# Scale after the product: RMSNorm's token factor moved behind the matmuls of a two-layer trunk

## The reference

```
def _rmsnorm(x, g):
    y = xf * lax.rsqrt(jnp.mean(xf * xf, axis=-1, keepdims=True) + RMS_EPS)
    return y * g
for layer in range(2):
    h = _rmsnorm(x, norm_mix[layer])
    if layer == 0:
        q, k, v, g, alr, u, sv = split(h @ even_w_in)        # 1024 -> 2576
        m = concat(_gla(q, k, v, g, alr, ...), _sgu(u, sv, ...))
    else:
        p = h @ odd_w_in                                      # 1024 -> 2720
        m = concat(_rwkv7(p[..., :1696], ...), _conformer_conv(p[..., 1696:], ...))
    x = x + m @ w_out
    f = square(relu(_rmsnorm(x, norm_ffn[layer]) @ w_up[layer]))   # 1024 -> 4096
    x = x + f @ w_down[layer]
return _rmsnorm(x, norm_final)
```

## Time and profile before

| | us |
|---|---|
| three runs | 1438.53, 1440.8, 1441.72 (median 1440.8) |
| the profiled execution: its own time | 1437.61 |
| the profiled execution: span of its trace | 1435.8 |
| PE busy | 1307.3 (91%) |
| DVE busy | 688.4 (48%) |
| ACT busy | 420.4 (29%) |
| POOL busy | 449.4 (31%) |

### The profile page before, as it was taken

One profiled execution on the slowest core, in us unless ns is written; L12 is line 12 of the kernel. 1 busy time (PEld: TensorE's weight loads), 2 busy tenths in 40 slices (PEclk: granted clock), 3 DMA queues, 4 the chain that ended last, 5 costly groups with the idle time before them and its releaser, 6 DMA issues. The chain is left out here.

```text
span 1435.8 us, 20378 instructions
## 1 busy us (share of the span) xinstructions
PE 1307.3 (91%) x8452; PEld 1046.4 (73%) x8452; DVE 688.4 (48%) x972; ACT 420.4 (29%) x535; POOL 449.4 (31%) x101
## 2 busy tenths in 40 slices
PE   4998998999999999898798898777889999999997
PEld 3897976888888888675666556564668888888885
DVE  6226256541014421386868878686655410144213
ACT  4537222231113211262435223232322311132110
POOL 3332232444434544321121110110224444345441
PEclk9999998999999999899999987898989999999998
DMA  5331212222232223201001000000022222322221
GB/s 191 121 108 34 86 59 88 75 100 89 90 106 97 88 91 110 93 30 60 31 31 59 30 31 2 30 31 1 30 88 78 98 88 91 108 93 88 92 85 58
DMA packets 16802, 106.17 MB, mean 74 GB/s; under 512 B 1872, under 2 KB 2144, under 8 KB 4704
## 3 DMA queue, kind: packets, MB, share of 16 engines
q1 hardware_dynamic: 15872, 103.83, 21.1%
q10 hardware_dynamic: 864, 1.36, 0.3%
HBM read 103.09 MB, written 2.10 MB: 73 GB/s over the span
## 5 line engine op out<-in xcount | busy, mean ns | idle before, releaser
L410 POOL TENSOR_TENSOR w_lo<-w_raw,w_hi 128x2048 fp32r<-128x2048 f32 x94 | 444.7, 4731 | 949.9 <-ACT w_hi L476 362.0
L748 PE MATMUL ps<-h_hi,w_hi 128*128 128x512 f32 x792 | 324.7, 410 | 8.5 <-DVE h_lo L1199 4.1
L748 PE MATMUL ps<-h_lo,w_hi 128*128 128x512 f32 x792 | 313.2, 395 | 0.0
L748 PE MATMUL ps<-h_hi,w_lo 128*128 128x512 f32 x792 | 312.8, 395 | 0.0
L748 PEld LDWEIGHTS ps<-h_hi,w_hi 128*128 128x128 f32 x792 | 151.2, 191 | 59.1 <-issue 19.9
L476 ACT ACTIVATE w_hi<-w_raw 128x2048 fp32r<-128x2048 f32 x58 | 111.1, 1915 | 276.5 <-PE ps L748 204.2
L748 PEld LDWEIGHTS ps<-h_hi,w_lo 128*128 128x128 f32 x792 | 151.4, 191 | 32.8
L748 PEld LDWEIGHTS ps<-h_lo,w_hi 128*128 128x128 f32 x792 | 151.7, 192 | 31.4 <-issue 2.7
L1253 DVE TENSOR_TENSOR x<-x,ps 128x512 f32 (+1 forms) x32 | 22.0, 687 | 305.2 <-PE ps L748 233.7
L1236 DVE TENSOR_TENSOR f_hi<-relu 128x512 f32 x64 | 71.6, 1119 | 172.2 <-ACT relu L462 160.3
L748 PE MATMUL ps<-f_hi,w_lo 128*128 128x512 f32 x384 | 151.9, 396 | 0.0
(11 more groups left out here) (279 smaller groups left out, 1769.3 us busy)
## 6 DMA issues: line engine op xcount, KB each, us to landing
w_raw<-in_weights SPq DMA_DIRECT2D x94, 1024.0 KB, 4.9
outT<-x SPq DMA_DIRECT2D x8, 256.0 KB, 2.2
x<-in_xT ACTq DMA_DIRECT2D x4, 256.0 KB, 5.5
x<-in_xT SPq DMA_DIRECT2D x4, 256.0 KB, 5.3
masks_f<-in_masks SPq DMA_DIRECT2D x1, 768.0 KB, 12.9
low_w<-in_low_w SPq DMA_DIRECT2D x1, 512.0 KB, 13.7
sgu_ln<-in_sgu_ln SPq DMA_DIRECT2D x1, 512.0 KB, 3.4
sgu_w<-in_sgu_w SPq DMA_DIRECT2D x1, 256.0 KB, 3.9
```

Source lines behind the costliest of these rows:

```text
L410: pool.tensor_tensor(w_lo[:, j, :], w_raw[:, j, :], w_hi[:, j, :].bitcast(f32), SUB)\
L748: mm = pe.matmul(bank(gb(g) if isinstance(i, int) else g % 2), w, r, start=(k == 0 and m == 0), stop=(k == K - 1 and m == 2))
```

## The change

The token factor is one number per token, so a product of (x times weight) differs from the product of the normed input by that factor alone. The changed kernel cuts x times weight: ACT makes `h_hi` straight from `x` with the weight as scale (`h_cut`), DVE `h_lo` in one instruction (`h_rest`), tile by tile as `x` becomes final. The factor is applied to the results: in the MLP as its square, since relu(c u) squared is c\*c relu(u) squared (`rn` then holds 1 / mean square, and DVE multiplies each down tile by it before adding it to `x`); in layer 0 as ACT's scale for the token-major tiles, and for k and q on the decay factors; in layer 1 at each tile's way out of PSUM, where the mix with `mu` is written anew (DVE `psh`, ACT `dsh` = psh times (1 - mu), DVE the sum). `stat` and `spread` become steps of the order, behind the first products. `m_hi0` to `m_lo1` give the mixers' outputs memory of their own, since `h_hi` is now written while an output product still reads its operands; other tensors move, and many counters are merged. In the first 13 tiles of layer 0 the PSUM banks come from a list (`FIRST_BANKS`). The first loads come in another order, and chunk 0 is loaded and cut only in its first half, which is all that its one product reads.

```
-        ORDER1 = [("slice", t, q) for q in range(4) for t in (0, 2)] + quarters([4])[:2] + [("zw", 0)] \
+        ORDER1 = [("slice", t, q) for q in range(4) for t in (0, 2)] + [("stat",)] + quarters([4]) + [("spread",)] \
...
-            if step[0] == "slice" and step[2] == 3 and (step[1] < 14 or step[1] % 2):
-                held += [("evac_v", step[1])]
-            if held and "dx" not in [other[0] for other in ORDER1[at + 1:at + 4]]:
-                order += held
-                held = []
+            if step[0] == "slice" and step[2] == 3:
+                held += [step[1]]
+            scaled_yet = scaled_yet or step[0] == "spread"
+            coming = [other[0] for other in ORDER1[at + 1:at + 4]]
+            if not scaled_yet or "dx" in coming:
+                continue
+            for t in begun:
+                order += [("evac_b", t), ("low", t)]
+            begun = []
+            for t in held:
+                order += [("evac_a", t), ("evac_q", t)]
+                if t == held[-1] and t < 14 and coming[:1] in (["slice"], ["taps"]):
+                    begun += [t]
+                else:
+                    order += [("evac_b", t), ("low", t)]
+            held = []
...
+            for k in (0, 2):
                 sp.dma_start(x[:, k, :], xT_in[:, k, :]).then_inc(s(f"x_loaded{k}"), 16)
-            for n in range(2):
-                sp.dma_start(w_raw[:, n, :], weights[n, :, :]).then_inc(s(f"raw_loaded{n}"), 16)
+            sp.dma_start(w_raw[:, 0, 0:1024], weights[0, :, 0:1024]).then_inc(s("raw_loaded0"), 16)
+            for k in range(4, KD):
+                sp.dma_start(x[:, k, :], xT_in[:, k, :]).then_inc(s(f"x_loaded{k}"), 16)
+            sp.dma_start(w_raw[:, 1, :], weights[1, :, :]).then_inc(s("raw_loaded1"), 16)
+            sp.dma_start(mats[:, :, :], mats_in).then_inc(s("mats_loaded"), 16)
             sp.dma_start(masks_f[:, :], masks_in).then_inc(s("masks_loaded"), 16)
             sp.dma_start(low_w[:, :, :], low_w_in).then_inc(s("low_w_loaded"), 16)
             sp.wait_ge(s("lo_done"), 1)
             sp.dma_start(w_raw[:, 0, :], weights[2, :, :]).then_inc(s("raw_loaded0"), 16)
-            sp.wait_ge(s("h_ready"), KD)
+            sp.wait_ge(s("stat_done"), 1)
...
+            pool.tensor_tensor(w_lo[:, 0, 0:1024], w_raw[:, 0, 0:1024], w_hi[:, 0, 0:1024].bitcast(f32), SUB)\
+                .then_inc(s("lo_done"), 1)
+            pool.wait_ge(s("hi_done"), 2)
...
+            def spread(m):
+                act.wait_ge(s("spread_done"), m + 1)
+                act.activation(rn[:, :], bank(6), ACT.Copy).then_inc(s("rn_done"), 1)
+            def h_cut(m, k):
+                if m:
+                    act.wait_ge(*x_final(m, k))
+                else:
+                    act.wait_ge(s(f"x_loaded{k}"), 16)
+                act.activation(h_hi[:, k, :], x[:, k, :], ACT.Copy, scale=col(NORMS[m], k)).then_inc(s("h_hi_done"), 1)
...
+                    elif layer == 0:
+                        for d in range(KD):
+                            if d < KD - 1:
+                                cut_hi(nd + 2 + d)
+                            h_cut(2, d)
+                        cut_hi(nd + 2 + KD - 1)
...
+            act.dma_start(cols[:, :], cols_in).then_inc(s("cols_loaded"), 16)
+            for k in (1, 3):
                 act.dma_start(x[:, k, :], xT_in[:, k, :]).then_inc(s(f"x_loaded{k}"), 16)
...
+            h_cut(0, 0)
+            h_cut(0, 1)
+            act.wait_ge(s("raw_loaded0"), 16)
+            act.activation(w_hi[:, 0, 0:1024], w_raw[:, 0, 0:1024], ACT.Copy).then_inc(s("hi_done"), 1)
+            for k in range(2, KD):
+                h_cut(0, k)
+            cut_hi(1)
...
+                act.wait_ge(s("gemm_done"), g + 1 + (g % 2 if kind == "v" else 0))
+                if kind == "v":
+                    act.wait_ge(s("rrms_done"), 1)
...
                 fn = {"v": ACT.Copy, "sv": ACT.Gelu_apprx_tanh, "u": ACT.Gelu_apprx_tanh, "g": ACT.Silu}[kind]
-                act.activation(dst[:, t, 256 * half:256 * half + 256], bank(g % 2, 0, 256), fn)\
-                   .then_inc(s(f"gemm_evac{g % 2}"), 1)
+                act.activation(dst[:, t, 256 * half:256 * half + 256], tok_bank(g), fn, scale=rrms[:, t:t + 1])\
+                   .then_inc(s(f"gemm_evac{g % 2}"), 2 if g == 2 else 1)
...
+            def out_cuts(m, n0):
+                for n in range(4):
+                    h_cut(m, 2 * n)
+                    h_cut(m, 2 * n + 1)
+                    cut_hi(n0 + n + 2)
+                load_sqrt(m)
+            out_cuts(1, N_OUT0)
...
+            def evac_q(t):
                 if t < 14:
                     i = [u for u in ROWS if u < 14].index(t)
...
+                    act.wait_ge(s("psh_done"), i + 1)
+                    act.wait_ge(s("zeroed"), 5)
+                    act.wait_ge(*evacuated(g1(t) - 1))
+                    act.activation(dsh[:, :], psh[:, i % 2, 1:SEQ + 1], ACT.Copy, scale=om_mu[:, i:i + 1])\
+                       .then_inc(s("dsh_done"), 1)
                 elif t % 2 == 0:
...
+                    act.wait_ge(*evacuated(g1(t)))
+                    act.activation(sgate[:, :], sgate[:, :], ACT.Sigmoid).then_inc(s("sgate_done"), 1)
...
                         first_up(lambda k: (s("h_ready"), 8 * m + k + 1))
+                        stat(m)
                         up(0, 1)
+                        spread(m)
...
+            def h_rest(m, k):
+                dve.wait_ge(s("h_hi_done"), 8 * m + k + 1)
+                stt(h_lo[:, k, :], x[:, k, :], col(NORMS[m], k), F(h_hi[:, k, :]), MUL, SUB).then_inc(s("h_ready"), 1)
...
+                    square(m, k)
+                    h_rest(m, k)
+                    add_square(m, k)
...
+                        g = gd + d
+                        dve.wait_ge(s("gemm_done"), g + 1)
+                        dve.wait_ge(s("x_half"), KD * (layer + 1))
+                        tt(scaled[:, d % 2, :], bank(g % 2), rn[:, :], MUL).then_inc(s(f"gemm_evac{g % 2}"), 1)
+                        dve.wait_ge(*evacuated(g))
+                        tt(x[:, d, :], x[:, d, :], scaled[:, d % 2, :], ADD).then_inc(s("x_done"), 1)
+                        square(m, d)
+                        if m == 2:
+                            h_rest(m, d)
+                        if m == 2 or d < KD - 1:
+                            add_square(m, d)
...
+            def alr():
+                dve.wait_ge(s("gemm_done"), 1)
+                dve.wait_ge(s("rn_done"), 1)
+                tt(alrT[:, :], rn[0:16, :], ps[0:16, 0, :], MUL).then_inc(s("alr_done"), 1)
...
+            def logb():
+                for c in range(2):
+                    dve.wait_ge(s("eend_done"), c + 1)
+                    tt(e_end[:, c, :], e_end[:, c, :], rn[:, :], MUL).then_inc(s("e_scaled"), 1)
+                    tt(e_neg[:, c, :], e_neg[:, c, :], rn[:, :], MUL).then_inc(s("e_scaled"), 1)
+                    dve.tensor_copy(e_last[:, c, :], e_pos[:, c, 63:SEQ:64]).then_inc(s("e_last_done"), 1)
+                for c in range(2):
+                    dve.wait_ge(s("e_last_done"), c + 1)
+                    tt(e_pos[:, c, :], e_pos[:, c, :], rn[:, :], MUL).then_inc(s("e_scaled"), 1)
...
+            def start():
+                norm(2)
+                ts(om_ka[:, :], cols[:, COLS["k_a"][0]:COLS["k_a"][0] + 4], -1.0, 1.0, MUL, ADD).then_inc(s("zeroed"), 1)
+                for i, t in enumerate([u for u in ROWS if u < 14]):
+                    one = ts(om_mu[:, i:i + 1], mu_col(t), -1.0, 1.0, MUL, ADD)
+                one.then_inc(s("zeroed"), 1)
+                dve.memset(psh[:, :, 0:1], 0.0).then_inc(s("zeroed"), 1)
+                dve.memset(SC[:, :, :], 0.0).then_inc(s("zeroed"), 1)
+                dve.memset(TX[:, :, :], 0.0).then_inc(s("zeroed"), 1)
+            def started():
+                dve.wait_ge(s("spread_done"), 3)
+                dve.memset(zpad[:, 0:TAPS - 1], 0.0).then_inc(s("zeroed"), 1)
+            def evac_a(t):
+                g = g1(t)
+                dve.wait_ge(s("gemm_done"), g + 1)
+                dve.wait_ge(s("rn_done"), 3)
+                if t < 14:
+                    i = [u for u in ROWS if u < 14].index(t)
+                    if i >= 2:
+                        dve.wait_ge(*evacuated(g1([u for u in ROWS if u < 14][i - 2])))
+                    tt(psh[:, i % 2, 1:SEQ + 1], rn[:, :], bank(gb(g)), MUL).then_inc(s("psh_done"), 1)
+                elif t % 2 == 0:
+                    dve.wait_ge(*evacuated(g - 1))
+                    tt(dsh[:, :], rn[:, :], bank(gb(g)), MUL).then_inc(s(f"gemm_evac{g % 2}"), 1)
...
-                    stt(dst[:, :], dsh[:, :], mu_col(t), bank(gb(g)), MUL, ADD).then_inc(s(f"gemm_evac{g % 2}"), 1)
+                    dve.wait_ge(s("zeroed"), 3)
+                    stt(dst[:, :], psh[:, i % 2, 0:SEQ], mu_col(t), dsh[:, :], MUL, ADD).then_inc(s(f"gemm_evac{g % 2}"), 1)
                 elif t % 2 == 1:
                     c = (t - 15) // 2
...
```

(6 more changed lines are left out.)

505 lines of the change are left out of this document (251 added, 254 removed).

## The result

The changed kernel took 1430.17 us (median of 5 runs, 1426.81 to 1433.71) against 1438.73 us before (5 runs); the ratio is 0.9934, 95% interval 0.991 to 0.9958. It is faster by 0.7%, 8.6 us where 24.9 were forecast, and the time lies just outside the range of 1402 to 1430. The profiled execution is the fastest one, 1426.81 us with a span of 1425.0; sums are made against the span before, 1435.8.

What follows compares the result with a forecast made beforehand. PE bounds the kernel, busy 91%, losing time at the joints, the start and layer 1's mixer. Terms -3 (start), -10.6, -4, -11.0 (norms 1 to 3), +3 (mixer), +0.7 (end) sum to -24.9: 1412.7 us profiled, 1416 median, range 1402 to 1430.

Steps and rivals of the forecast that it cites:

- Norms 1 and 3: Joints ahead of the MLPs' up tiles: PE no longer waits, each takes 13.5 us, saving 10.6 and 11.0 us.
- Norm 2: Joint ahead of layer 1's mixer: first scores 2.3 or 6.7 us earlier, taken as 4 (0 to 8).
- The case in which nothing is held: At norm 2, no small DVE instruction held by POOL: first mix 20.3 us behind the MLP's end, scores 6.7 us earlier.
- Layer 1's mixer: Stretch from the first scores on: added DVE work half hides, the rest delays PE; +3 us, bounds -1 and +20.
- the hop: Layer 1's mixes going DVE, ACT, DVE: DVE's 0.6 us wait for ACT was said to cancel against an earlier wait.
- The added DVE work: Layer 1's gate tiles and second `zpad` passes: 5.5 us more on DVE, of which half hides.
- Rival 2: DVE becomes the bound of layer 1's mixer part way: +13 instead of +3, time 1426; chance 0.13.
- Rival 3: Slower: layer 1's mixes pay ACT's answers, added instructions and POOL's holds, 60 us in all, time 1472; chance 0.06.
- Rival 4: Joints stay, PE waiting for the eighth tile or weights: norms 1 and 3 gain 3 each, 1431; chance 0.05.
- The start: Way to layer 0's k: first product near 11.2 us, but held sums delay the chain; k at 58.3, gain 3.
- plus 1 for the lower clock: At the start, 1 us added to k's start at 58.3 for PE's lower clock after its waits.
- The end: The program's last down tile openly pays one more DVE product: +0.7 us.

Runs made afterwards that it cites:

- e1: Changed kernel with the load of chunk 3 issued ahead of `alpha_w`; 1425.80 us, ratio 0.992 to before.
- e12: Changed kernel with full subtractions, its mix adding `psh` itself without ACT's pass, factor (1 - mu) left out; 1419.77 us, ratio 0.9863.
- e8: e4 with the mix adding `psh` itself, without ACT's pass, factor (1 - mu) left out; one run, 1387.67 us.
- e3: Changed kernel with the token factor left out of the eight convolution gate and value tiles, 8 DVE instructions less; ratio 0.9899 to before.
- e9: e4 with the token factor left out of the eight gate and value tiles, as in e3; one run, 1404.70 us.
- e5: Kernel before, with POOL's 12 subtractions in layer 1's mixer and output product cut to 64 columns; ratio 0.9777 to before.
- e4: Changed kernel with POOL's 12 subtractions in layer 1's mixer and output product cut to 64 columns; ratio 0.978 to before.
- e6: Changed kernel with the edits of e1 and e2, and four masked `sgu_w` copies moved behind `alrT`; 1414.4 us, ratio 0.9841 to before.
- e10: e6 with POOL's 12 subtractions in layer 1's mixer and output product each made in four instructions of 512 columns; 1397.72 us, ratio 0.9718.
- e2: Changed kernel with the factor applied before the products again in layer 1's mixer only; 1421.69 us, ratio 0.9885 to before.

## Why the prediction was wrong

- **Norms 1 and 3** were right in mechanism and size: forecast 13.5 us for each joint; with the sums (0.95) and the spread (1.05 us) norm 1 takes 13.3 (11.3 without them). The allowance of 0.5 for a late bank wasn't needed. Norm 3 lost 2.2 us to a held `f_lo`: I had given DVE's part of an up tile no chance to run over, though `f_lo` frees a bank and a hold is 5 us. The stall stands in six of thirteen profiles of the changed kernel and its variants.
- **Norm 2** came to -3.8 for -4, and the match is partly luck. The case in which nothing is held came true (the first mix at 19.5 us behind the MLP's end, 20.3 forecast), for which 6.7 us were written down; -4 was a mean of two cases. The same code gave -6.5 in e1, with PE's busy time 3.0 us shorter.
- **Layer 1's mixer** holds the step that failed: "Each mix also has DVE wait for ACT (0.6), where before DVE waited for ACT's copy ahead of it, which cancels." It doesn't. Before, ACT's copy waited for PE (and for a buffer freed two tiles earlier), and ran ahead of DVE. Now ACT waits for DVE in the middle of its queue, and the chunk's pieces, `TX` and `U` behind it wait too; then DVE waits for ACT. Taking the hop away gives back 6.8 of the 9.3 us of PE's idle time that the change added to the mixer (e12), and 7.4 of 10.2 with POOL out of the way (e8); by length it is worth 9.7 us from the first MLP's end to the end of output product 1 with full subtractions, and 17.4 without (441.0 to 423.5), the difference being for the most part PE's busy time at other granted clocks. The hop was priced at zero. The forecast for this stretch and the next was +3, and they took +10.9.
- **The added DVE work** ("half of the added time hides; the rest lands") was near: leaving the gates' passes out gives back 1.8 us of PE's idle time (e3) where some 3 us were forecast, and nothing when POOL is out of the way (e9).
- **Rival 2** (+13 in the mixer, time 1426) comes nearest in size, but by another mechanism: it had DVE as the bound, and DVE's busy time in the stretch rose by 0.7 us only.
- **Rival 3**, a slower time by the same mechanism in full, had ACT's answer at 1.3 us for each of 10 mixes and holds as a price on top. The first part was nearly the case. The holds were not on top: POOL's nine subtractions add 22.9 us to DVE's busy time before (259.4 against 236.6 in e5) and 19.1 in the changed kernel (260.1 against 241.0 in e4).
- **Rival 4** gave 1431, close to the time measured, with joints that stay. They are gone, so that is chance.
- **The start** was walked right to 0.7 us up to the decays' product; the term "plus 1 for the lower clock" was mis-sized: at a mean granted clock of 0.69 the way to k took 10.9 us for 7.7 at full clock. k stands at 60.9 to 62.9 us in seven profiles of this code (62.1 and 63.9 before), so a gain of 0.9 is about what they show. It was lost again by the end of output product 0: from k on the changed kernel took 169.7 us where the one before took 168.1, but e5, the same code as before there, took 169.5, and the changed code up to 173.1.
- **The end** cost 1.9 for 0.7: PE waits 1.45 us for the last squares instead of 0.72, and its granted clock falls some 2.4 us behind the MLP's end instead of 4.0, so that the last products run at the 1.2 GHz level. e6 and e9, with the same end, took 14.0 us, 0.6 more than before: the 0.7 forecast was right, and the rest goes with this execution's clock.

## What to carry to other kernels

Before an elementwise pass is put on another engine, ask what it waits for: here a pass that waited for PE ran ahead in its queue, and one that waited for DVE stopped the queue for what stood behind it. And where two engines exclude each other, cut the instructions of the one that has slack into short ones: a long one holds whatever comes second to its end. When one profile of each kernel is compared, split the stretch into PE's idle and PE's busy time first: here the idle time came back within 0.1 us for the same code, and the busy time moved with the granted clock enough to hide most of a gain or to double one.

## What the hardware showed beyond what was expected

Holding goes both ways: POOL's subtraction took 6.00 us beside DVE's squares in the changed kernel, which end 1.6 us behind its start, where 4.62 us stand in the mixer, and a piece of 512 columns 1.51 us beside a busy DVE. The Trainium skill ("SBUF — State Buffer", section "Who interferes with whom") has the order of issue decide who blocks, for the whole instruction; these rows agree, and e10 is what shorter instructions are worth in this kernel, 16 us in layer 1.

What holds cost in all was more than thought: 34 us from the first MLP's end to the end of output product 1 before (457.9 to 423.5, e5), of them 11 ahead of the scores. 23.0 of the 34 are PE's idle time; in the other 11 the same products run at a mean granted clock of 0.94 instead of 0.91.

The clock differs between executions of the same code. Here 120 to 140 us, first in the changed kernel, then in e12, which has the same code there but reached k 1.7 us later:

```profile
120.00:140.00 20.00, 17.66 (x194) 15.06 (x193) 11.26 (x20) 13.65 (x17) 3.37 (x1) 1.00 0.16 54
```

```profile
120.00:140.00 20.00, 17.65 (x172) 14.30 (x171) 10.01 (x19) 12.68 (x17) 1.42 (x1) 0.83 0.15 53
```

Layer 0 from k to the transposes ahead of its output product takes 121.0 to 124.5 us in profiles of one and the same code there. What decides it stays open.

The output products run slightly slower with their operands in memory of their own: 0.227 us for a matmul before, 0.231 to 0.233 changed, 0.6 to 0.9 us for the last 144 of layer 0's 192. It can be at most 0.7 of the 2.7 us behind layer 1's mixer: e2, e6 and e12 took 61.0 to 61.3 us there, and the kernel before 60.7. Why was not tried.
